# Two norms moved beside linears, weights split two pieces ahead, and the output stored by tiles, in a three-layer kernel on one core

## What is computed

```python
def first_block(...):
    hn = rms_norm(h, norm_mix_g)
    proj = hn @ w_in                                   # linear in1: conv_a | conv_gate | ssm_u
    yc = conformer_conv_group(conv_a, conv_gate, ...)  # conv, layer_norm, c * sigmoid(c)
    ys = s5_group(ssm_u, ...)                          # z = gelu(y); z * sigmoid(z @ glu_w)
    y = concatenate([rms_norm(yc, grp_norm_conv_g), rms_norm(ys, grp_norm_ssm_g)])
    h = h + y @ w_out                                  # out1
    mem_n = rms_norm(mem, mem_norm_g)
    h = h + mem_cross_attention(rms_norm(h), mem_n, w_q, w_kv, w_o)   # query1, o1
    h = h + peer(rms_norm(h), ...)                     # experts
```

## Time and profile before

| | before |
|---|---|
| median of 3 runs | 4378.3 us (4376.87 to 4382.64) |
| profiled execution | 4380.69 us, its span 4379.0 |
| PE busy | 3958.6 us, 90% |
| DVE busy | 2579.7 us, 59% |
| ACT busy | 1632.4 us, 37% |
| POOL busy | 90.3 us, 2% |
| mean granted PE clock | 0.953 |
| DMA | 650.22 MB, 148 GB/s |

### The profile page before, as it was taken

How to read it: one execution, slowest core, us unless ns; L and a number is a source line. 1 busy time by engine, 2 the same in 40 slices (tenths; PEclk the granted TensorE clock), 3 DMA queues, 4 the chain that set the end, 5 groups by cost and what they waited for, 6 DMA issues and landing times. The chain is left out here.

```text
span 4379.0 us, 66086 instructions
## 1 busy us (share of the span) xinstructions
PE 3958.6 (90%) x24860; PEld 3518.4 (80%) x24860; DVE 2579.7 (59%) x3858; ACT 1632.4 (37%) x2076; POOL 90.3 (2%) x133
## 2 busy tenths in 40 slices
PE   8887889988569999999999999898998778999989
PEld 8774489986358888888888888897997778898889
DVE  5577845446786556565565655543795654565454
ACT  4204334341135444454454443433442113343343
POOL 0001100000000000000000000000000000000000
PEclk9988999998799999999999999998998898999999
DMA  6333345352246565665656655454341004543334
GB/s 233 115 111 106 110 141 167 116 165 97 95 179 209 186 211 186 210 206 187 211 185 208 208 187 181 143 177 154 117 139 38 1 0 139 162 144 122 117 118 159
DMA packets 182955, 650.22 MB, mean 148 GB/s; under 512 B 24856, under 2 KB 27288, under 8 KB 180384
## 3 DMA queue, kind: packets, MB, share of 16 engines
q1 hardware_dynamic: 180528, 626.06, 43.7%
q0 software_dynamic: 2016, 19.92, 1.2%
q10 hardware_dynamic: 144, 0.52, 0.0%
HBM read 623.35 MB, written 23.09 MB: 148 GB/s over the span
## 5 line engine op out<-in xcount | busy, mean ns | idle before, releaser
L2346 DVE TENSOR_TENSOR dense_weights_trailing<-weight_ring,dense_weights_leading 128x1024 fp32r<-128x1024 f32 x512 | 624.3, 1225 | 560.4 <-ACT dense_weights_leading L2310 559.5
L2310 ACT ACTIVATE dense_weights_leading<-weight_ring 128x1024 fp32r<-128x1024 f32 x512 | 538.5, 1058 | 683.0 <-PE dense_down L2300 357.7
L2278 PE MATMUL dense_up<-pe_parts,dense_weights_leading 128*128 128x512 f32 x2048 | 720.1, 399 | 24.0 <-DVE dense_weights_trailing L2346 14.7
L2300 PE MATMUL dense_down<-dense_weights_leading,dense_act_parts 128*128 128x512 f32 x2048 | 630.6, 389 | 0.0
L2278 PE MATMUL dense_up<-pe_parts,dense_weights_trailing 128*128 128x256 f32 x2048 | 553.2, 280 | 0.0
L2278 PEld LDWEIGHTS dense_up<-pe_parts,dense_weights_leading 128*128 128x128 f32 x2048 | 378.5, 188 | 116.5 <-issue 22.0
L2300 PEld LDWEIGHTS dense_down<-dense_weights_leading,dense_act_parts 128*128 128x128 f32 x2048 | 384.4, 188 | 79.5
L2300 PE MATMUL dense_down<-dense_weights_trailing,dense_act_parts 128*128 128x512 f32 x1024 | 398.3, 389 | 0.0
L2278 PEld LDWEIGHTS dense_up<-pe_parts,dense_weights_trailing 128*128 128x128 f32 x2048 | 387.2, 189 | 10.1
L510 PE MATMUL lin_out_acc<-lin_out_parts,lin_out_weights_leading 128*128 128x256 f32 x1792 | 327.8, 286 | 29.2 <-DVE lin_out_weights_trailing L403 29.2
L403 DVE TENSOR_TENSOR lin_in_weights_trailing<-weight_ring,lin_in_weights_leading 128x1024 fp32r<-128x1024 f32 x176 | 216.2, 1232 | 172.1 <-ACT lin_in_weights_leading L398 170.1
(11 more groups left out here) (725 smaller groups left out, 7530.5 us busy)
## 6 DMA issues: line engine op xcount, KB each, us to landing
weight_ring<-in_w_experts SPq DMA_DIRECT2D x512, 512.0 KB, 4.3
weight_ring<-in_w_in SPq DMA_DIRECT2D x176, 512.0 KB, 3.4
weight_ring<-in_w_out SPq DMA_DIRECT2D x112, 512.0 KB, 4.2
weight_ring<-in_w_att SPq DMA_DIRECT2D x64, 512.0 KB, 4.2
weight_ring<-in_w_gate SPq DMA_DIRECT2D x40, 512.0 KB, 3.3
weight_ring<-in_w_key SPq DMA_DIRECT2D x32, 512.0 KB, 3.3
weight_ring<-in_w_value SPq DMA_DIRECT2D x32, 512.0 KB, 3.3
weight_ring<-in_w_query SPq DMA_DIRECT2D x32, 512.0 KB, 3.4
```

What stands on the lines that cost most here:

```text
L2278: mm = nc.tensor.matmul(to, still, moving, start=begin and m == 0, stop=end and m == 1)
L2300: mm = nc.tensor.matmul(down[:, bank, t], still, moving, start=begin and m == 0, stop=end and m == 2)
L2310: nc.scalar.activation(ring.leading[:, b], ring.ring[:, b], ACT.Copy).then_inc(split_led, 1)
L2346: v.tensor_tensor(ring.trailing[:, b], ring.ring[:, b], ring.leading[:, b].bitcast(F32), ALU.subtract).then_inc(ring.split, 1)
```

## The change

Five edits. (1) The first memory's norm no longer is a stage: `MemoryNormBeside` runs it beside `in1`; the wait for its load goes there too, and the tiles of `in1` are now all written out. (2) `causal_conv` ends with its last tap; layer norm, silu and group norm of its result run beside the gate linear (`ConvolvedBeside`), with column sums in place of sums by rows, the bias within the silu, and the silu by chunks. (3) Split slots may be held across stages (`ring.hold`), and a linear with `ahead=2` splits the first two pieces of the next one behind its own last pieces; the next linear waits for its features alone there. Ten linears find two pieces split: `out1`, `query1`, `o1`, `dv2`, `in2`, `in3`, `upk`, `upv`, `gate3` and `out3`. (4) The last level of the delta rule leaves out `ps_b` and `x`, which nothing reads. (5) The last linear stores its output by tiles.

The ring and `linear`:

```diff
+        self.held, self.holds, self.begun = 0, False, 0
...
     def split_slots(self, s):
 
+        if self.holds:
+            return
...
-def linear(k, ring, src, dst, residual=False, tokens=False, parts=None, norm=None, fetch=None, beside=None):
+def linear(k, ring, src, dst, residual=False, tokens=False, parts=None, norm=None, fetch=None, beside=None, ahead=0, store=None):
...
+    begun, ring.begun = ring.begun, ahead
...
+                if store is not None:
+                    for n in range(tiles):
+                        sp.wait_ge(taken, n + 3)
+                        sp.dma_start(store[:, 4 * n:4 * n + 4], dst[:, 4 * n:4 * n + 4]).then_inc(stored, 16)
+                    sp.wait_ge(stored, 16 * tiles)
...
                         pe.wait_ge(ring.split, g + 1)
+                        if first_tile(n) and split_here and c < begun:
+                            pe.wait_ge(featured, c + 1)
...
+                        if not first_tile(n) or c >= begun:
+                            act.wait_ge(ring.landed[b], ring.landings(n, per, first + c))
+                            if not isinstance(n, int) or g >= slots:
+                                act.wait_ge(ring.freed, g - slots + 1)
+                            splitter.on_scalar(act, ring.ring[:, b], ring.leading[:, b])
...
+                for c in range(ahead):
+                    g, b = next_piece(c)
+                    act.wait_ge(ring.landed[b], (g // slots + 1) * 16)
+                    act.wait_ge(ring.freed, g - slots + 1)
+                    splitter.on_scalar(act, ring.ring[:, b], ring.leading[:, b])
+                    if other:
+                        next(turns, None)
...
+                            if c < begun:
+                                ins.then_inc(featured, 1)
                         b = piece(n, c)[1]
-                        splitter.on_vector(dve, c * (leads + 1) + leads if first_tile(n) else n * per + (leads * per + c),
-                                           ring.ring[:, b], ring.leading[:, b], ring.trailing[:, b]).then_inc(ring.split, 1)
+                        if not first_tile(n) or c >= begun:
+                            led = c * (leads + 1) + leads if first_tile(n) else n * per + (leads * per + c)
+                            splitter.on_vector(dve, led - skipped(n, c), ring.ring[:, b], ring.leading[:, b],
+                                               ring.trailing[:, b]).then_inc(ring.split, 1)
...
                         if other:
-                            if not first_tile(n) and c == slots:
-                                take(n - 1, 1 - half)
+                            turn = n * per + c - slots
+                            if turn > 0 and turn % per == 0:
+                                take(turn // per - 1, (turn // per - 1) % 2)
...
+                for c in range(slots):
+                    if c < ahead:
+                        b = next_piece(c)[1]
+                        splitter.on_vector(dve, tiles * per + leads * per + c - begun, ring.ring[:, b], ring.leading[:, b],
+                                           ring.trailing[:, b]).then_inc(ring.split, 1)
+                    if other:
+                        turn = tiles * per + c - slots
+                        if turn > 0 and turn % per == 0:
+                            take(turn // per - 1, (turn // per - 1) % 2)
                         next(turns, None)
                         next(finishing, None)
                 take(tiles - 1, (tiles - 1) % 2)
```

Beside the linears (the sums of the memory's norm are two matmuls a turn, from the twelfth piece on):

```diff
+    def on_scalar(self, act):
+        yield from idle(self.START)
+        act.wait_ge(self.here, self.count)
+        for g in range(DC // 2):
+            if g >= 2:
+                act.wait_ge(self.summed, g - 1)
+            self.k.nc.scalar.activation(self.sq[:, g % 2], self.h[:, 2 * g:2 * g + 2], ACT.Square).then_inc(self.squared, 1)
+            yield
+        yield
+        yield
+        self.inverse.on_scalar(act)
+    def on_tensor(self, pe):
+        yield from idle(self.START + 1)
+        for g in range(DC // 2):
+            pe.wait_ge(self.squared, g + 1)
+            for j in range(2):
+                mm = self.k.nc.tensor.matmul(self.banks[:, 2, 0:SEQ], self.k.const("ones"), self.sq[:, g % 2, j],
+                                             start=g + j == 0, stop=g == DC // 2 - 1 and j == 1)
+            mm.then_inc(self.summed, 1)
+            yield
+    def on_vector(self, dve):
+        ch = Chain(dve, self.step)
+        yield from idle(self.START + 1 + DC // 2)
+        dve.wait_ge(self.summed, DC // 2)
+        self.inverse.average(dve, ch, self.banks[:, 2, 0:SEQ], DM)
+        yield
+        self.inverse.refine(dve, ch, self.scale[:], self.inverted)
+        yield
+        dve.wait_ge(self.inverted, 1)
+        for c in range(DC):
+            self.k.nc.vector.scalar_tensor_tensor(out=self.h[:, c], in0=self.h[:, c], scalar=self.gain[:, c:c + 1],
+                                                  in1=self.scale[:], op0=ALU.mult, op1=ALU.mult)
+            if c % 4 == 3:
+                yield
...
+    def on_tensor(self, pe):
+        self.sum(pe, 0, self.out).then_inc(self.totaled, 1)
+        yield
+        yield
+        for n in range(2):
+            pe.wait_ge(self.squared, n + 1)
+            self.sum(pe, 1 + n, self.sq).then_inc(self.summed, 1)
+            yield from idle(5)
+    def on_scalar(self, act):
+        nc, half = self.k.nc, self.chunks // 2
+        yield
+        for n in range(2):
+            if n == 0:
+                act.wait_ge(self.centered, 1)
+            else:
+                act.wait_ge(self.summed, 1)
+                act.wait_ge(self.open, 2)
+            for c in (0, half):
+                ins = nc.scalar.activation(self.sq[:, c:c + half], self.out[:, c:c + half], ACT.Square)
+            ins.then_inc(self.squared, 1)
+            yield
+            yield
+            self.inverses[n].on_scalar(act)
+            yield
+            if n == 0:
+                yield
+                for c in range(self.chunks):
+                    if c % half == 0:
+                        act.wait_ge(self.normed, c // half + 1)
+                    ins = nc.scalar.activation(self.out[:, c], self.out[:, c], ACT.Silu, bias=self.k.col("conv_ln_b")[:, c:c + 1])
+                    if c % half == half - 1:
+                        ins.then_inc(self.open, 1)
+                        yield
+    def on_vector(self, dve):
+        k, v, half = self.k, self.k.nc.vector, self.chunks // 2
+        ch = Chain(dve, self.step)
+        dve.wait_ge(self.totaled, 1)
+        ch.then(v.tensor_scalar(self.mean[:], self.banks[:, 0, 0:SEQ], 1.0 / D_CONV, None, ALU.mult))
+        v.tensor_tensor(self.out, self.out, self.mean[:].unsqueeze(1).to_broadcast([P, self.chunks, SEQ]),
+                        ALU.subtract).then_inc(self.centered, 1)
+        yield
+        yield
+        for n, gain in enumerate((k.col("conv_ln_g"), k.col("grp_norm_conv_g"))):
+            dve.wait_ge(self.summed, n + 1)
+            self.inverses[n].average(dve, ch, self.banks[:, 1 + n, 0:SEQ], D_CONV)
+            yield
+            self.inverses[n].refine(dve, ch, self.scale[:], self.inverted)
+            yield
+            dve.wait_ge(self.inverted, n + 1)
+            for c in range(self.chunks):
+                ins = v.scalar_tensor_tensor(out=self.out[:, c], in0=self.out[:, c], scalar=gain[:, c:c + 1], in1=self.scale[:],
+                                             op0=ALU.mult, op1=ALU.mult)
+                if c % half == half - 1:
+                    ins.then_inc(self.normed, 1)
+                    yield
+            yield
```

Where they are called:

```diff
 def mixing(k, ring, h, y, proj, key, value):
 
     with k.nc.sbuf_tensor("mix_scale", [P, SEQ], F32) as scale, k.nc.semaphore("mem_here") as mem_here:
         linear(k, ring, k.x, proj, norm=Norm(k.col("norm_mix_g"), scale), fetch=(mem_here, [
-            (k.consts[:, FIRST_CONSTS:], k.args["consts"][:, FIRST_CONSTS:]), (k.rows, k.args["rows"]), (h, k.args["mem_t"])]))
-        wait_for(k, mem_here, 48)
-    feature_norm(k, h, DC, k.col("mem_norm_g"), h)
+            (k.consts[:, FIRST_CONSTS:], k.args["consts"][:, FIRST_CONSTS:]), (k.rows, k.args["rows"]), (h, k.args["mem_t"])]),
+               beside=lambda s, taken: MemoryNormBeside(k, s, h, k.col("mem_norm_g"), mem_here, 48))
     conv, ssm = y[:, 0:8], y[:, 8:16]
     causal_conv(k, ring, proj, conv, h, key)
-    feature_norm(k, conv, 8, k.col("grp_norm_conv_g"), conv)
     state_space(k, ring, proj[:, 16:24], ssm, h, value)
...
-    linear(k, ring, ssm, glu)
+    ring.hold(k.held)
+    linear(k, ring, ssm, glu, ahead=2, beside=lambda s, taken: ConvolvedBeside(k, s, conv))
...
     with k.nc.sbuf_tensor("ca_scale", [P, SEQ], F32) as scale:
-        linear(k, ring, k.x, h, norm=Norm(k.col("norm_mem_g"), scale))
...
-        linear(k, ring, y, k.x, residual=True)
+        ring.hold(rest)
+        linear(k, ring, y, k.x, residual=True, ahead=2)
...
```

(25 more changed lines are left out.)

139 lines of the change are left out of this document (69 added, 70 removed).

## The result

The changed kernel takes 4328.9 us (median of 4 runs, 4326.7 to 4330.5) against 4380.5 for the kernel before, run beside it; the ratio is 0.9875, 95% interval 0.9864 to 0.9887. The forecast was 4320 with the range 4305 to 4335. The profiled execution took 4328.19 us with a span of 4326.5, so 52.5 us less than before by the spans, where the sum said 57.9. Of the 8.9 us by which the forecast was too low, 5.4 are this sum. Most of the rest is the step from the profiled execution to the median: the forecast took off 2.4 us there, and the median came out 0.7 above the profiled execution.

What follows compares the result with a forecast made beforehand. TensorE was taken to bound the linears, with engines taking turns in short chains between. Savings of 12.4 + 16.9 + 16.6 + 8.8 + 3.2 = 57.9 us took 4380.7 to 4322.8, less 2.4 for the median: 4320, range 4305 to 4335.

Steps and rivals of the forecast that it cites:

- The memory's norm: The norm moved beside `in1`: 21.3 us of stage removed, 8.86 us of TensorE sums added, minus 12.4 us.
- the 8.86 us for the sums: TensorE's 16 sums, 32 passes, moved into `in1`; since TensorE never waits there, 8.86 us added in full.
- The convolution's norms: Norms moved beside the gate linear: 42.9 us removed, that stage 26 us longer, minus 16.9 us.
- The three table loads: Extra ScalarE loads in the gate linear's chain, 1.28 us each; the skill's drain, left out, would add up to 4.1 us.
- ScalarE takes the root only behind the split of the eighth piece: Gate linear: after that split and a 1.28 us table load, the root is placed at 28.0 us from stage start.
- 20 if the root comes early: Lower bound, in us, on the gate linear's lengthening, forecast at 26; the upper bound was 34.
- Two pieces ahead: Ten linears find two pieces split; earlier TensorE starts shift their ends, except `upk` with nothing: minus 16.6 us, bounds 8 and 25.
- The last level and the store: Delta rule's last level: 2.2 us in four chunks, minus 8.8; output stored by tiles: minus 3.2 us.
- A (clock stays up): Rival: three or four of ten starts keep the higher clock, each giving 2 to 3 us: 4311 us, chance 0.15.
- B (the rise comes at the same moment): Rival: starts gain only half and the gate linear's sums run at the lower clock: 12 less gain, 4332 us, chance 0.12.
- C (more waits in the gate linear): Rival: the chain in the gate linear finds more waits than placed: 10 us more, 4330 us, chance 0.10.
- D (last takes behind pieces that had not landed): Rival: at each linear's end the last take waits for DMA behind the next linear's splits: slower, 4393 us, chance 0.015.

## Why the prediction was right, and where it was off

**The memory's norm: mechanism right, one size off.** No wait appeared in `in1`, and the forecast 158 us were 156.3. The failing number is the 8.86 us for the sums. It is the time of 32 passes in a stage at mean clock 0.78, and it was carried over into a stage at 1.00, where 7.0 was measured: 1.9 us, the whole miss of this part. The row with the clock was in the same view and was not used here, while the same clock was used for the rivals.

**The convolution's norms: right, step by step.** 27.5 us longer against 26, within the bounds of 20 to 34. The three table loads beside: each is 1.28 long, and the first is followed by its activation after 0.02 (506.28 + 1.28, 507.58). The Trainium skill, "ScalarE: Activation LUTs", section "What ACT_TABLE_LOAD costs", adds a drain of about 1.38 us; this trace shows none at that load, and the stage came out at the forecast length without it. The others lay in ScalarE's waits. What the forecast did not see is that its own step "ScalarE takes the root only behind the split of the eighth piece" was a choice of the order, worth 7.3 us: 4.9 for the root itself and 2.4 because the second sums then run at the full clock. The bound "20 if the root comes early" was the right idea: with the root early the stage is 20.2 us longer than before.

**Two pieces ahead: the step that failed.** "In all of them TensorE is the bound behind the start, so a shift at the start is a shift of the end" is false for `in2`. There TensorE's second turn waits for VectorE's multiply behind the fifth split, and that split's piece landed no earlier for being asked for 2 us earlier, behind the 1536 KB that SyncE issues first. The start moved by 2.34, from 2.65 to 0.31 us; the narrow products started at 12.46 as before, and took 1.4 us longer behind the longer wait. So a gain of 2.4 came out as a loss of 1.4, the largest single miss. Against the kernel with no piece ahead the stage gained nothing either; there the piece landed 1.8 us earlier, so part of the growth of the wait from 0.28 to 3.77 is that. The step also missed the cost on the other side: VectorE's idle 8.84 before the last take was taken as cover for all linears, but in the gate linear the same change had just filled that time with the norms' chain (3.9 us with all pieces gone, 2.9 with its own alone, of which 2.2 to 2.3 are the two splits). At the other starts the shifts, against the kernel with no piece ahead, were worth roughly what was forecast: `query1` 2.4 (forecast 1.8), `in3` 2.1 (1.8), `out1` 1.4, `o1` 1.5 and `out3` 0.6 (1.6 each), `dv2` 2.5 and `upv` 2.0 (1.7 each), `gate3` 1.4 (2.4), `upk` 0.8 (0). For `in3` and `gate3` this is luck as much as agreement: alike kernels differ there by 2.5 and 2.7 us. In all the part measured 12.0 where 16.6 was forecast, within its bounds of 8 to 25.

**The last level and the store** came out at 7.6 and 4.0 against 8.8 and 3.2. For the store the row of 3.4 us was that of the weights under load; the last quarter took 3.0 from issue to the end of the span. The Trainium skill's fit ("DMA: Bandwidth & Descriptors", section "Anatomy of one DMA — SWDGE (gpsimd) path") gave an estimate of 3.2, nearer than the row, though it is a fit for GpSimd's queue and these stores go by SyncE's. The median for the four stores is 6.1, longer than the 3.8 of the weights in the same stretch, but only the last one is waited for.

**The rivals.** A (clock stays up) happened in part: at the start of `query1` the mean clock of 10 us went from 0.66 to 0.83, so at the lower of the two levels it spent 3.4 of them and no longer 6.8. B (the rise comes at the same moment) held for `out3`, where the clock rose 6.9 us behind the stage's start before and 7.1 now and 0.6 to 0.8 of 1.6 was left, and for `out1`, where it rose at 7.4 and 7.2 and 0.9 was left against before. Its other half, the second sums at the lower clock, held too: 6.11 us at a mean clock of 0.60, inside the 4.3 to 6.5 that the forecast allowed. C (more waits in the gate linear) was wrong as put: the waits were those laid out. D (last takes behind pieces that had not landed) never happened at a stage's end, but its mechanism, a piece that lands later than the engines want it, is what took the gain in `in2`: at the start, not the end.

What stays open: why `in2` varies between 279 and 286 us among kernels in which it is alike. The length follows the clock: over the first 45 us its mean is 0.79 in the profile of 279.2 us, 0.75 in two of 282.3 and 0.66 in that of 286.1. What makes it fall for longer or shorter no run set apart.

## What to carry to other kernels

When a stage is made to start earlier, look for the next thing in it that is tied to a fixed moment (a transfer that the stage's own start issues, above all), for what stands in front of it in its queue, and for what is queued behind it on the engines. Moving what need not wait ahead of it was tried here; moving the transfers was not. When a chain is laid beside a linear, the place of each handover among the linear's own waits is worth as much as the overlap itself: put the step that another engine waits for ahead of the engine's wait, not behind. A few products of no use, no longer than the gap that they fill, can pay for themselves where TensorE stands idle for 3 us between two dense stages, but look at the stage behind too, which may give part of it back.

## What the runs showed of the hardware that was not expected

Closing a gap of a few us kept the granted clock up, but the gap alone does not tell the clock. At `query1` TensorE had been idle for 4.88 us before, 3.19 in the changed kernel and 1.65 with the added products; the mean clock of the first 10 us was 0.66, 0.83 and 1.00, and with the products it was 1.00 over the whole of `query1` and `o1` in all four kernels. Yet with the same 3.19 us it was 1.00 with the convolution's norms as before, and 0.66 where the gate linear splits nothing ahead:
```profile
671.74:681.74 10.00, 8.30 (x66) 8.22 (x67) 8.24 (x13) 9.87 (x20) 3.59 (x4) 1.00 0.48 168
...
652.16:662.16 10.00, 8.29 (x47) 8.25 (x48) 8.08 (x13) 9.86 (x20) 2.33 (x3) 0.66 0.52 177
```
Both differ from the changed kernel only in work that lies about 100 us and more ahead of `query1`; no run tells what of it decided.

A transfer that is asked for earlier need not land earlier. The fifth piece of `in2` was issued 0.6 us behind the stage's start instead of 2.5 and landed at 9.5 in both cases, behind a load of 1536 KB issued at 0.12.

A product of 128x128 by 128x256 in plain f32 cost 0.46 to 0.49 us at the full clock (1.97 us for four, 3.69 for eight, two records of the profile each). The linear's products of the same shape, in the rounded f32 type, take a quarter of the time: 768 of them in the 95.8 us of `o1`, 0.12 us each. The cost of filler has to be taken from a row of the same type, and by products, not by passes.

Kernels that are alike in a stage differ there by a few us, and mostly by about the same amount: the norm ahead of `att2` took 19.1 or 20.8 us in most profiles, the head norm 15.1 or 16.7, `dv2` 46.7 or 48.3. The clock goes with it: the head norm has a mean clock of 0.66 wherever it took 15.1 us and 0.59 wherever it took 16.7, `dv2` 1.00 at 46.4 to 46.7, 0.96 at 48.3 and 0.93 at 50.6. What decides it between kernels that are alike up to there is not settled. For parts worth under 7 us the stage of the profile told more than medians of four runs.
